# Two-layer hybrid sequence model: the second layer's modulation placed in the output of the first layer's last tile

## What is computed

```python
def hybrid_layer(x, c, pos0, k_buf, v_buf, shift_prev, wkv0, conv_buf, h0, lp):
    mod = jax.nn.silu(c) @ lp["w_mod"] + lp["b_mod"]          # [1024] @ [1024, 3072]
    shift_m, scale_m, gate_m = jnp.split(mod, 3, axis=-1)
    h = rmsnorm(x, lp["norm_pre"]) * (1.0 + scale_m[:, None]) + shift_m[:, None]
    proj = h @ lp["w_in"]                                     # [1024, 2880]
    ya = swa_banded(...) if k_buf is None else swa_cached(...)   # windowed attention
    yb, shift_new, wkv_new = rwkv7_time_mix(...)              # recurrent, chunked
    yc, conv_new, h_new = rglru_mix(...)                      # convolution and gated recurrence
    y = jnp.concatenate([ya, yb, yc], axis=-1) @ lp["w_out"]  # [1024, 1024]
    x = x + gate_m[:, None] * rmsnorm(y, lp["norm_post"])
    return x, (k_new, v_new, shift_new, wkv_new, conv_new, h_new)
```

## Time and profile before

| | us |
|---|---|
| median of 3 runs | 2910.8 |
| lowest and highest run | 2907.3, 2911.91 |
| profiled execution | 2903.72 |
| its span in the profile | 2901.9 |
| PE busy in the span | 2757.8 (95%) |
| DVE, ACT, POOL busy | 1720.0, 1338.5, 255.2 |
| DMA moved | 119.18 MB, 41 GB/s in the mean |
| mean granted TensorE clock | 0.969 of full speed |

### The profile page before, as it was taken

How to read it: one execution, slowest core, us unless ns; L and a number is a source line. 1 busy time by engine, 2 the same in 40 slices (tenths; PEclk the granted TensorE clock), 3 DMA queues, 4 the chain that set the end, 5 groups by cost and what they waited for, 6 DMA issues and landing times.

```text
span 2901.9 us, 63519 instructions
## 1 busy us (share of the span) xinstructions
PE 2757.8 (95%) x25044; PEld 2016.0 (69%) x25044; DVE 1720.0 (59%) x4641; ACT 1338.5 (46%) x3128; POOL 255.2 (9%) x357
## 2 busy tenths in 40 slices
PE   6999999999999999997769999999999999999976
PEld 5777777777777777775457777777777777777753
DVE  1666666666666666665416666665666666666654
ACT  1545444544554444443215544445445554444432
POOL 0010111101101011100001000111011100011000
PEclk8999999999999999999769999999999999999997
DMA  9200000000000000000660000000000000000001
GB/s 341 97 16 24 23 24 23 9 24 24 24 24 17 23 24 23 16 9 22 206 243 16 19 22 23 24 23 17 16 24 24 24 20 21 24 23 16 16 19 33
DMA packets 55176, 119.18 MB, mean 41 GB/s; under 512 B 15312, under 2 KB 27216, under 8 KB 54608
## 3 DMA queue, kind: packets, MB, share of 16 engines
q1 hardware_dynamic: 52912, 114.28, 11.5%
q10 hardware_dynamic: 1952, 0.48, 0.1%
HBM read 96.34 MB, written 18.41 MB: 40 GB/s over the span
## 4 chain that ended last, share of the span: by engine, by line
PE 91%; DVE 4%; DMA 2%; issue 1%; ACT 1%; SPq 0%; POOL 0%; DVEq 0%; POOLq 0%; ACTq 0%
PE G L468 17%; PE G L576 16%; PE M L792 15%; PE G L463 8%; PE M L463 5%; PE M L625 5%; PE M L459 4%; PE M L638 3%; PE G L693 2%; PE G L474 2%; DMA RB<-in_w_mod 2%; PE M L604 1%; PE M L674 1%; PE G L459 1%; DVE Q L1441 1%
## 5 line engine op out<-in xcount | busy, mean ns | idle before, releaser
L468 PEld LDWEIGHTS G<-hT,w_in 128*128 128x128 f32 x4224 | 495.2, 194 | 21.9 <-issue 16.5
L468 PE MATMUL G<-hT,w_in 128*128 128x128 f32 x4224 | 507.1, 278 | 3.3 <-issue 3.3
L576 PE MATMUL G<-hT,w_in 128*128 128x256 f32 (+1 forms) x2048 | 497.1, 385 | 0.0
L792 PE MATMUL M<-w_out,yT 128*128 128x512 f32 x1024 | 452.8, 596 | 5.8 <-DVE yT L1579 5.8
L576 PEld LDWEIGHTS G<-hT,w_in 128*128 128x128 f32 x2048 | 360.4, 189 | 64.7 <-issue 12.3
L792 PEld LDWEIGHTS M<-w_out,yT 128*128 128x128 f32 x1024 | 193.4, 191 | 225.2 <-issue 223.7
L463 PE MATMUL G<-w_in,hT 128*128 128x512 f32 x512 | 244.4, 610 | 0.0
L1441 DVE TENSOR_TENSOR Q<-Q,M 64x256 f32<-64x256 f32 x320 | 133.8, 418 | 130.5 <-PE M L638 127.3
L625 PEld LDWEIGHTS M<-W 64*64 64x64 f32 x4608 | 147.7, 135 | 24.3 <-issue 24.3
L625 PE MATMUL M<-W 64*64 64x64 f32 x4608 | 162.7, 219 | 0.0
L1231 POOL TENSOR_TENSOR RA<-RA,small 128x1024 f32<-128x1024 f32 x32 | 60.6, 1895 | 1136.9 <-DVE small L1493 1136.9
(11 more groups left out here) (413 smaller groups left out, 4562.7 us busy)
## 6 DMA issues: line engine op xcount, KB each, us to landing
w_in<-in_w_in SPq DMA_DIRECT2D x8, 2048.0 KB, 15.1
RA<-in_w_mod SPq DMA_DIRECT2D x16, 512.0 KB, 6.9
W<-in_w_mod SPq DMA_DIRECT2D x16, 512.0 KB, 6.9
xa<-in_x_prompt SPq DMA_DIRECT2D x16, 512.0 KB, 3.7
w_out<-in_w_out SPq DMA_DIRECT2D x2, 4096.0 KB, 18.4
G<-in_x_prompt SPq DMA_DIRECT2D x16, 512.0 KB, 3.5
x_mid<-RA SPq DMA_DIRECT2D x16, 512.0 KB, 2.9
xa<-x_mid SPq DMA_DIRECT2D x16, 512.0 KB, 3.6
```

The lines of the kernel that those rows point to most:

```text
L468: last = mm(out[0:width, :], Win[:, k, col:col + width], H[:, k, :], start=k == 0, stop=k == KC - 1)
L576: last = mm(out, Win[:, k, col:col + P], moving, start=k == 0, stop=k == KC - 1)
L792: last = mm(o[:, :], yT[:, k, :], Wout[:, k, 512 * h:512 * h + 512], start=k == 0, stop=k == KC - 1)
```

## The change

1. Modulation of layer 1: its 24 chunks are loaded and multiplied in the output of layer 0's last tile. Chunks go through six other buffers (`wnext`: xa, both halves of hT, half of RA, the tensor KB that holds kr and bk, RB), into the PSUM tensors `MB`, and ACT copies the rows (`mod_row`) and the folded channels (`mod_copy`, into `modr`). SP issues the first six loads behind six different events of the last tile and the others as chunks are consumed. DVE pads the condition into `cnext` inside that tile.
2. PE's order in that tile: chunks 0 to 5 before `ynT`; 6, 7 and fold 0 before `project(0)`; then the sample's sum of squares, chunks 8 to 11, fold 1, 12 and 13; `project(1)`; chunks 14 to 23 and folds 2 to 5.
3. The sample's input norm (`sample_input`) is made inside the last tile of both layers, before the residual on DVE, with its sum between the two projections on PE.
4. The six writes of the final states go from SP's queue to ACT's, after `o_ready`. In layer 0 DVE's clearing of the states (`cleared`), which waits for them, stands behind the sample's first row copy.
5. The opening of layer 1 up to `h_hi` stands in layer 0's sample stage; `modulation(1)` too; xa is loaded behind the sample's `y`, `load_small(1)` is issued by ACT there.
6. The x of tile 1 of each layer comes by a buffer of its own (`x2`, over KB), is squared after `copy_rk` and scaled before the token shift.
7. The parameters `prm` and `spc` hold both layers; both softplus chains run after layer 0's modulation.
8. At the start the condition and the first five chunks are loaded before the constants, which come in fewer DMAs, partly on ACT's queue. The gate columns C_GB are an own piece of `w_in` (`win_gb`), loaded earlier and filled before `front`.
9. The sample's row copies go to `srow` (xs, qk) instead of hT; one wait of PE (`kT_ready`) is dropped; the constants ms and mst change places, so the mask of one Gram product is a view of blocks 0 and 2 of three.

The diff, cut to what the prediction speaks of:

```diff
+        wnext = [flat(xa[:, :]), hT[:, :, 0, :], flat(RA[:, 0:1024]), flat(KB[:, :, :].rearrange("p a b -> p (a b)")),
+                 hT[:, :, 1, :], flat(RB[:, :])]
+        x2 = KB[:, :, :].rearrange("p a b -> p (a b)")
...
+        MB = (M0, M1, G0, M2, M0, M1)
...
+            sp.dma_start(cst[:, 0:2 * P], d["cst"][:, 0:2 * P]).then_inc(L["const"], 16)
+            sp.dma_start(qk[:, 0:384], d["masks"]).then_inc(L["const"], 16)
...
+                if mixed:
+                    m = NT - 1
+                    sp.wait_ge(s["xT_hi"], DONE(m))
+                    load_next(0)
+                    sp.wait_ge(s["gbc_mm"], DONE(m - 1))
+                    load_next(1)
+                    sp.wait_ge(s["pT1_mm"], DONE(m))
+                    load_next(2)
+                    sp.wait_ge(s["y_mm"], DONE(m))
+                    sp.dma_start(xr, rows(src, m)).then_inc(L["xr_in"], 16)
+                    load_next(3)
+                    sp.wait_ge(s["gbc_mm"], DONE(m))
+                    load_next(4)
+                    sp.wait_ge(s["pv_mm"], DONE(m))
+                    load_next(5)
+                    for q in range(NWM, 24):
+                        load_next(q)
+                    sp.wait_ge(s["o_ready"], DONE(m))
+                    sp.dma_start(rows(dst, m), ob).then_inc(L["y_out"], 16)
+                    sp.wait_ge(L["mod_mm"], 48)
+                else:
+                    residual_and_store(NT - 1, l * NT + NT - 1)
...
+                if mixed:
+                    load_x2(d["x_mid"][P:2 * P, :])
+                    sp.wait_ge(L["modT_mm"], 1 + MODG)
...
+                    sp.wait_ge(smp["dve"], AT("y", l))
+                    sp.dma_start(xa[:, :], d["x_mid"][0:P, :]).then_inc(L["x_in"], 16)
+                    load_rope(0, (l + 1) * NT)
...
+                def mod_chunks(*qs):
+                    for q in qs:
+                        g, j = q // 4, q % 4
+                        pe.wait_ge(wmod_in[q % NWM], 64 + (q // NWM + 1) * 16)
+                        column_groups(MB[g][:, P * j:P * j + P], cnext, lambda k: wnext[q % NWM][:, k, :])\
+                            .then_inc(L["mod_mm"], 1)
+                def mod_fold(g):
+                    pe.wait_ge(L["mod_act"], MROW[g])
+                    for j in range(4):
+                        last = mm(MB[g][:, 9 * j:9 * j + 9], mrow[g % 2][:, P * j:P * j + P], fold[:, 0:1 + B], start=True,
+                                  stop=True)
+                    last.then_inc(L["modT_mm"], 1)
...
+                    fused = mixed and not ahead
+                    if fused:
+                        pe.wait_ge(L["padded"], 2)
+                        mod_chunks(0, 1, 2, 3, 4, 5)
...
+                        mod_chunks(6, 7)
+                        mod_fold(0)
...
+                    else:
+                        pe.wait_ge(smp["dve"], AT("sq", l))
+                        for k in range(KC):
+                            last = mm(M3[:, 0:B], con("reset")[:, 1:2].to_broadcast([P, P]), dsq[:, k, :], start=k == 0,
+                                      stop=k == KC - 1)
+                        last.then_inc(smp["pe"], 1)
+                    if fused:
+                        pe.wait_ge(s["gbc_out"], DONE(n))
+                        mod_chunks(8, 9, 10, 11)
+                        mod_fold(1)
+                        mod_chunks(12, 13)
                     project(1, M4).then_inc(s["o1_mm"], 1)
-
-                x_lo(l * NT)
-                x_hi(l * NT)
+                    if fused:
+                        mod_chunks(14, 15)
+                        mod_fold(2)
+                        pe.wait_ge(L["mod_act"], MFOLD[0])
+                        mod_chunks(16, 17, 18, 19)
+                        mod_fold(3)
+                        pe.wait_ge(L["mod_act"], MFOLD[1])
+                        mod_chunks(20, 21, 22, 23)
+                        mod_fold(4)
+                        mod_fold(5)
...
-                front(l * NT)
-                pe.wait_ge(L["win"], (l + 1) * 64)
+                pe.wait_ge(L["win_gb"], (l + 1) * 16)
                 pe.wait_ge(s["rk_out"], DONE(l * NT))
                 for j in range(4):
                     last = channels(G0[:, P * j:P * j + P], hT[:, :, 0, :], C_GB + P * j, P)
                 last.then_inc(L["g0_mm"], 1)
+                front(l * NT)
+                pe.wait_ge(L["win"], (l + 1) * 48)
...
+                    x_lo((l + 1) * NT)
                 pe.wait_ge(smp["dve"], AT("osq", l))
                 for k in range(KC):
                     last = mm(M4[:, 0:B], one, dsq[:, k, :], start=k == 0, stop=k == KC - 1)
                 last.then_inc(smp["pe"], 1)
+                if mixed:
+                    x_hi((l + 1) * NT)
...
+                copy_rk(l * NT)
+                x_square(l * NT + 1, hT[:, :, 1, :], 1)
+                for step in (copy_wka, copy_v, low_rank):
                     step(l * NT)
-                x_square(l * NT + 1, hT[:, :, 1, :])
                 act.wait_ge(L["g0_mm"], l + 1)
                 A(stBC[:, 0], G0[:, :].rearrange("p (c t) -> p c t", c=4), ACT.Copy).then_inc(L["g0_out"], 1)
+                decays(l * NT)
...
+                act.wait_ge(s["o_ready"], DONE(l * NT + NT - 1))
+                for out, carry in ((d["k_p"], kT[:, 0:P]), (d["v_p"], Vt[:, 0, :]), (d["shift_p"], pB[:, :, 0]),
+                                   (d["wkv_p"], S[:, 0, :, :]), (d["conv_p"], xcb[:, :, 0:3]), (d["h_p"], hcar[:, :])):
+                    act.dma_start(out[l], carry, allow_slow_non_contiguous=out is d["shift_p"]).then_inc(L["state"], 16)
...
+                if mixed:
+                    act.wait_ge(L["mod_mm"], 48)
+                    x_square((l + 1) * NT, hT[:, :, 1, :], -1)
+                    act.wait_ge(L["mod_out"], 2)
+                    act.wait_ge(L["zeros"], 2)
+                    h_lo((l + 1) * NT, hT[:, :, 0, :])
...
-                    mask = cst[upper, o:o + 2 * CH].rearrange("p (w c) -> p w c", w=2)
+                    mask = cst[upper, o:o + 3 * CH].rearrange("p (w c) -> p w c", w=3)[:, 0::2]
...
+                    else:
+                        sample_input()
...
+                dve.wait_ge(s["xT_hi"], DONE(l * NT))
+                x_mean(l * NT + 1, x2)
+                dve.wait_ge(L["prm"], 32 + (l + 1) * 128 + 48)
...
+                    cp(srow[g % 2][:, 0:width], (G1, G0)[g % 2][:, 0:width]).then_inc(L["row_out"], 1)
+                    if mixed and g == 0:
+                        cleared(l + 1)
...
+                    dve.wait_ge(L["mod_act"], MFOLD[5])
+                    modulation(l + 1)
```

410 lines of the change are left out of this document (233 added, 177 removed).

## The result

The changed kernel takes 2873.4 us in the median of four runs (2870.89 to 2876.68), beside 2909.05 for the kernel before (2903.54 to 2911.91, four runs): 0.988 of its time, 95% interval 0.9861 to 0.99. That is 35.6 us between the medians and 28.6 us between the two profiled executions (2903.72 and 2875.11, spans 2901.9 and 2873.3). The direction was forecast; 2873.4 lies 15.4 above the predicted 2858 and 1.4 above the range.

The account below looks back on a forecast made before the run. PE works nearly without a gap in the tile loops, so the change acts at the seams. Gains of 33.5 (middle), 6.3 (start), 5 (openings) and 8.3 (end) sum to 53.1: 2910.8 becomes 2858 us, range 2846 to 2872.

Parts of the forecast that it names:

- step 2: Layer 0's sample stage: DVE's clearing waits for the six state writes and PE behind it, 9.6 us lost, bounds 0 and 13.
- rival (a): State writes in layer 0 land before PE needs the row: 8.5 us less, 2849; chance 0.2.
- I take 13: Layer 0's six state writes: 13 us assumed from first issue to last landing, so all in at 1403.
- The bound of 13 us: Layer 0's sample stage: most that PE could lose to the state writes, if the sample's own loads slow them.
- step 1: Layer 0's last tile: modulation chunks put there make the sample's first column group 6.9 us later, at best 5, at slow price 13.
- Rival (b): Tail stays at the slow chunk price, 2865, or layer 1's x comes late, same size; chance 0.25 together.
- step 3: Sample chain to layer 1: fill_rk at 1470.7 against 1504.24, w_in and x not binding; middle gains 33.5 us.
- step 4: Kernel start: w_mod issued earlier, load-paced stage moves by 5.6 us; 6.3 gained in all, 4 to 8.
- step 5: Opening of each layer: gate columns cover the xs wait, L595 nearer to v; 2.5 us gained per layer, 0 to 3.7.
- step 6: Kernel end: column groups follow the last projection at once, first channels earlier; 8.3 us gained, 6 to 9.
- rival d: Loop tiles: strided mask slows a DVE pair in each tile, kernel slower than before, some 2915 to 2920; chance 0.04.
- a state wait at its upper bound: High end of the range, 2872: the slow chunk price in the tail together with PE's state wait at 13 us.

## Why the prediction was right or wrong

**The new wait (step 2): right in kind, wrong in size by 12 us.** It was forecast that DVE would wait for all six writes in `cleared(1)`, that PE would wait for DVE, and that this would cost more than it seems because row groups follow on a cold PE. All of it is in the rows, the kernel without the wait shows its price, and rival (a), that the writes don't bind, is out. Two sizes failed. The first, 7.7 of the 12.2 us, is the flight of the writes: the step "I take 13" from first issue to last landing. 13.1 is what they take with the loads held, but here SP issued the sample's loads in the same microseconds, from 3 us ahead of the first write, and 20.9 us came of it. In the trace of before these loads stood behind the writes in one queue. (The end of the kernel was misread besides: 2824.12 to 2838.4 is 14.3, not 13.6.) The text had this as a possibility ("the sample's own loads, issued in the same microseconds, slow them") and put it into the bound instead of into the value. The bound of 13 us for PE's loss was too small as well: PE lost 14.8. That the writes sit on ACT's queue, which rival (a) counted in their favour, did not keep the loads on SP's from slowing them.
The second, 4.7 us, is the price of the low clock: 12 us were taken for the row groups behind the pause, and they took 16.7, at 0.50 of full speed up to 1424. This size is not fixed. Behind waits of 11.9, 13.6 and 14.7 us in other profiles they took 16.5, 14.4 and 12.2, so the 12 was within what can come. What lets the upper level return sooner is not shown. From the first column group to the end of the proj rows it was 39.2 us, forecast 27.0.
The figure of the Trainium skill that was weighed there ("DMA: Bandwidth & Descriptors", "Anatomy of one DMA", some 2.0 us fixed and the bytes over 436 GB/s, for the GpSimd path) would have given, as an estimate, a stall of 3. In the profile with packed writes and held loads PE waited 1.8 and DVE 3.9, and a 64 KB write took 1.6 to 2.2 us where that sum gives 2.2; for the writes as the kernel has them, with PE waiting 11.9 and 14.8, it was wrong by 9 us or more.

**The tail (step 1): half right.** Warm chunks took 0.62 to 0.65 each and started 0.44 to 0.46 apart (forecast 0.61), the projection 7.1, the sum of squares 1.85 instead of 3.55 ("about 2"), and the norm of the sample did vanish under the second projection. But the first column group came 11.6 us later relative to the start of the tail, forecast 6.9. Two steps failed. The first is "about 1.3 us each ... so the fifth lands near 1352.0", which is 1347.0 on the time of this profile. The five loads issued from 1337.90 to 1342.34 landed at 1341.4, 1345.1, 1346.5, 1348.1 and 1349.9. The second of them, the residual's x, is already 2.4 us behind: it took 5.9 us where a lone load takes 3.5,

```profile
G<-in_x_prompt SPq DMA_DIRECT2D x1, 512.0 KB, 5.9
```

and the others follow 1.4 to 1.8 apart. From 1339 to 1346 the DMAs moved 259 GB/s and over the eight microseconds from 1342 319, where the 397 of the earlier trace rows were taken; why so little isn't shown. Two more loads (issued at 1342.9 and 1343.4, as the buffers of chunks 0 and 1 are free) share the stream from there on. `ynT` was 3.3 us later than forecast, but shorter projections and chunks gave back 2: the second projection ended 1.5 later than forecast.
The larger part, 3.2 of the 4.7, came behind it. Chunks 20 to 23 were forecast to land 3.5 us after their issue and 1.3 apart; they took 3.7, 4.7, 5.0 and 6.4. PE waited 2.5 us in all, fell to the low clock, and the last folds took 3.58. The store of the tile (512 KB, issued at 1379.86) is in flight beside the last two, which the forecast left out; no run parts its share.
Rival (b), the slow price throughout, did not come: from 1355 to 1380 the clock was at its upper level. It came at both ends of the tail.

**The chain (step 3): right.** From the proj rows to the end of the output's row channels 48.8 us, forecast 48.9; from there to `fill_rk` 4.7, forecast 5.3; `w_in` and x bound nothing. Of the middle's 33.5 us, 17.3 came: 12.2 of the difference are the wait and what follows it, 4.7 the tail.

**The start (step 4): 3.2 instead of 6.3.** The first w_mod was issued at 1.32 (forecast 1.6), but the last chunk came at 43.40, only 2.9 before that of the earlier trace rows. The step that failed is "the stage is paced by the loads, so it moves by 5.6":

```profile
13.33 1.08 PE L512 MATMUL G<-G,yT 128*32 128x128 f32 x16 [2.78 <-DMA qk<-in_masks]
18.50 1.08 PE L512 MATMUL G<-RB,yT 128*32 128x128 f32 x16 [4.09 <-DMA RB<-in_w_mod]
...
43.40 0.70 PE L512 MATMUL G<-RB,yT 128*32 128x128 f32 x16 [1.72 <-DMA RB<-in_w_mod]
...
53.00 9.53 PE L506 MATMUL G<-hT,w_in 128*128 128x128 f32 x64 [1.64 <-issue]
```

It is paced by the loads, but by all of them. The first chunk ran 7.1 us earlier than before (6.12, 13.27 before), chunk 5 only 2.2 (18.50, 20.67) and the last one 2.9, so the rest was lost between the first chunk and chunk 5. PE waits there 2.78 for the masks, a constant that now travels behind the first w_mod and is still due before the chunk in G, which itself was in 1.3 us earlier, and 4.09 for the chunk in RB (chunk 5), which stands behind x and the second x in SP's list. "Pays 1.5 for the x of tile 1 and constants" had the right kind and too small a size: two executions with that x behind the chunks put it alone at about 2 us, and the masks come on top. In the mean of eleven executions with this start 3.3 us were gained against the one profile of before, so the profiled one is no outlier.

**The openings (step 5): 2.3 and 0.7 instead of 2.5 each.** The mechanism stood as forecast, a wait of "some 4 us" for `h_lo` of tile 1, measured 4.86, and the order itself brought 1.4 us in each layer. What was too small is the term behind that wait: "then needs 7.6 for the rest", or 9.1 with the clock low, where layer 1 took 9.5 to the bonus. So the bonus came 24.9 and 25.3 us behind v, forecast 22.5 to 24. What layer 0 has over that and layer 1 gave back lies in the fill ahead: 9.53 us in layer 0, 10.20 before, and 10.15 in layer 1, where the earlier trace rows had 9.84. This was read from one execution each.

**The end (step 6): 5.5 instead of 8.3.** The first channels start 6.0 us after the projection's end, about as forecast. The projection's two halves and the sum between them took 17.9 us, forecast 17.2, as the first half took 9.27; from the first channels to the end of the proj rows it was 14.4 instead of 12.7, as one column group took 3.55 where the next of its size took 1.92; and the chain after them took 0.6 more than before. The first two are rows on the low clock behind a pause of PE, 2.81 us ahead of the projection and 2.52 ahead of the first channels.

**The loops (rival d): right that nothing happens.** From the bonus of layer 1 to the last projection the gain stays at 23.1. The strided mask costs nothing that shows.

**In all.** Of some 24.6 us missing against the sum of 53.1, 12.2 are the wait for the states, 4.7 the tail, 3.1 the start, 2.8 the end, 2.0 the openings. Taking the clearing out of the way gives back 18.7 and none of the other kernels is told from that one as faster (0.9823 of before). The range failed by its upper end: "a state wait at its upper bound" was there with too low a bound.
That the median missed by 15.4 and not by 24.5 is luck. The forecast carried along that the median of before lay 7.1 us above its profiled execution; the profiled execution of the changed kernel lies 1.7 above its median. These two, 8.8 us together, have nothing to do with the mechanism. They also bound what the table of stretches can tell: it compares one execution with one, and two executions of the same kernel differ by up to 3 us at a single mark.
Three sums of the prediction are off by 0.5 to 0.7 and change nothing: the 13.6 named above, the end of projection 1 (its own terms add up to 1379, not 1378.5), and the 49.9 us of the old modulation stage, where the 33.5 gained and the 6.9 and 9 paid add up to 49.4.

## What to carry to other kernels

A wait for the landing of small writes belongs where nobody stands behind it; ahead of the next use of the buffer, not at the place where the writes happen to be issued. When a DMA's time is taken from a row of the trace, look at what else was in flight at that row and what will be in flight at the new place; if the two differ, the difference goes into the value and not into the bound. A pause on TensorE is to be priced with what follows it: here 11.9 to 14.8 us of waiting were followed by row groups 2.3 to 6.8 us longer than without it, 17 to 22 us in all.

When chunks go through a few buffers, the place of a chunk decides when the load so many places on may start; moving one behind a long operation brings the wait back later. Neither of the two other orders tried here made the tail shorter.

## What the hardware showed that was not expected

- A write of 3.5 KB in 896 single elements took 9.0 us with no loads beside it, the same bytes in 128 runs of 28 bytes 1.5. A 64 KB write issued behind the first took 9.0, behind the second 2.2.
- Writes on ACT's queue and loads on SP's slow each other: the last unpacked write took 13.4 to 19.4 us in layer 0, where the loads are issued first (eight profiles), 10.7 to 12.4 at the end of the kernel, where the first write is (ten profiles), and 10.2 without loads; the load of `wkv_s` (512 KB) 18.7 us beside unpacked writes, 8.6 beside packed ones, 6.3 and 5.4 after them.
- Even with both removed, a 1 KB write at the end of six took 5.0 us from its issue, while the 64 KB ones took 1.6 to 2.2. Why isn't settled; `conv_p` (12-byte runs) right before it took 3.0.
- After the 14.8 us pause PE stayed on the low clock from 1411 to 1424 (0.50), though it was busy for 12.3 of these 13 us. In another execution, after a pause of 14.7 us, the same row groups had the upper level from 1419 on (1.00). What makes the difference isn't settled.
- Two executions of one kernel put the start of the tail 3 us apart (chunk 2 at 1343.12 and 1346.25), with nothing to choose between them but the first modulation stage and layer 0's opening. A single look at a mark that late can't judge an edit of 2 us; the length of the stretch around the edit can.
